# Long convolution by token parity: 256 frequencies for both halves of the spectrum, and two input-projection blocks behind the forward transforms

## Chip, cores and metric

The kernel runs on one NeuronCore of a Trainium2 chip. The metric is the device time of one execution, in microseconds.

## What is computed

A two-layer hybrid trunk runs over 128 context and 512 latent tokens (640 columns). Each layer has one input projection whose columns go to four branches: latent attention (A), a bidirectional gated delta rule (B), a long convolution (C) and differential attention (D). A gated merge and an MLP follow. The change lies in branch C:

```python
def _hyena_branch(u, conv_w, conv_b, filt, d_bias):
    uc = _dwconv_centred(u, conv_w) + conv_b
    x0, x1, v = jnp.split(uc.astype(f32), 3, axis=-1)
    v = v * x1
    h_fwd, h_bwd = filt[:, :HY_W], filt[:, HY_W:]
    h_circ = jnp.concatenate([h_fwd, jnp.zeros((1, HY_W), f32), jnp.flip(h_bwd[1:], axis=0)], axis=0)
    n_fft = 2 * seq
    y = jnp.fft.irfft(jnp.fft.rfft(v, n=n_fft, axis=1) * jnp.fft.rfft(h_circ, n=n_fft, axis=0), n=n_fft, axis=1)[:, :seq]
    return ((y + v * d_bias.astype(f32)) * x0).astype(u.dtype)
```

There are 256 channels. Latents (512 tokens) and context (128) are separate sequences.

## The kernel before, in words

Each engine has its own program, written by hand; semaphores (`signal(...)`, waited on with `.nth(l, n)`) join them, and the order of the code is the order of the work. Both layers run in one loop of depth 2.

The input projection is cut into 24 blocks of 128 output columns. `win_block(l, n)` waits for the block's weights in a ring of four slots (SyncE loads them), then makes 8 x 2 matmuls over all tokens into bank pair `psD[:, n % 2]` of PSUM. Blocks 0 to 5 are the convolution's x0, x1 and v; blocks 6 to 11 are the delta rule's q, k and v. ScalarE copies a block to one of two stages (`evac_conv`), and VectorE makes the short convolution from it (`conv`).

`hyena(l)` of TensorE is the stage in question. Between the first blocks it makes the filter network (L786, L791) and the filter's five token tiles (`windowed`, L776), which VectorE multiplies by a decay window (L1919) and turns into a sum and a difference of the two directions. After block 5 come:

- `gate_input_rows` (L756), small matmuls for the delta rule's gates
- the filter's transform (L811, context L814): for each of five tiles of frequencies and for cosine and sine, matmuls over the token tiles; ScalarE scales each result (L1541, L1542)
- `gate_inputs` (L764), the turning of the values, tokens to partitions (L823), which ScalarE copies out (L1544), and the sums with alternating signs, that is the one frequency at the middle of the circle (L832), whose product VectorE makes (L1944)
- the values' transform (L843, L846); for each tile VectorE makes the complex product with the filter's spectrum (L1951 to L1954)
- the inverse (L854 to L859) into `psD`, with the middle frequency as a term of one row (L856, L859)
- VectorE adds `v * d` and multiplies by x0 (L1960, L1963) and signals `hyena_done`, for which TensorE waits ahead of block 6, since the delta rule's buffers lie over the convolution's in the arena.

Then `gdn(l)` takes blocks 6 to 10 and goes on with the delta rule. GpSimd has nothing to do in the stage. It sends the tables (`dft`) to the arena at the layer's start.

Of the kernel before, what the change touches and what calls it, by code (L numbers as in the profile page):

```python
# [101 lines left out]
DFT, DFT_W = layout([("cs", 4 * 2 * LAT), ("csp", 2 * CTX), ("win", NT * 512), ("z", T)])  # L102
# [5 lines left out]
DVE_LINKS = 225  # L108
# [26 lines left out]
def trunk(nc, ins, outs, links):  # L135
    ctx = ExitStack()
    with ctx:
# [70 lines left out]

        cv = Carve()
# [4 lines left out]
        hspec = cv(NT, 3, 256)  # L214
        yspec = filt
        hprod = cv(2, 512)
        hnyq = cv(2, 256)
        hmul = cv(512)

        sarg, sn, ssin = (hspec.rearrange("p a b c -> p (a b c)")[:, i * T:(i + 1) * T] for i in range(3))  # L220
        dcs = dft[:, 0:4096].rearrange("p (k c f) -> p k c f", k=4, c=2)
        dcsp = dft[:, 4096:4352].rearrange("p (c f) -> p c f", c=2)
        win = dft[:, 4352:4352 + 2560].rearrange("p (t c) -> p t c", t=NT)
        zf = dft[0:33, 4352 + 2560:4352 + 2560 + T]
# [11 lines left out]
        def flat_bout(n):  # L236
            return bout[:, n].rearrange("p c t -> p (c t)")

# [78 lines left out]
        hspec_ps = signal("hspec_ps", NT)  # L317
        hspec_ready = signal("hspec_ready", NT)
        vspec_ps = signal("vspec_ps", NT)
        yspec_ready = signal("yspec_ready", NT)  # L320
        nyq_ps = signal("nyq_ps", 1)
        nyq_ready = signal("nyq_ready", 1)
# [116 lines left out]
        pool_chain = signal("pool_chain", 0)  # L439

        def halves(ap):

            return ap.rearrange("p (s n) -> p s n", s=2)

# [88 lines left out]
        def _(pool):  # L533
# [6 lines left out]
            with pool.Fori(0, DEPTH) as l:  # L540
# [5 lines left out]
                pool.dma_start(x_kept, x[:]).then_inc(x_out.sem, 16)  # L546

# [139 lines left out]
        def _(pe):  # L687
# [64 lines left out]
            def gate_input_rows(l):  # L752

                for k in range(KC):
                    for a, b in SEGS:
                        last = mm(psD[32 * (k % 4):32 * (k % 4) + 32, 0, a:b], p_("wab")[:, k * 32:(k + 1) * 32],  # L756
                                  h[:, k, a:b], start=k < 4, stop=k >= 4)
                last.then_inc(ab_rows_ps.sem, 1)

            def gate_inputs(l):  # L760

                pe.wait_ge(*ab_rows_in.nth(l, 1))
                for t in range(NT):
                    last = mm(psD[:, 0, 768 + t * 16:768 + (t + 1) * 16], ab_rows[:, t * P:(t + 1) * P], c_("pick"),  # L764
                              start=True, stop=True)
                last.then_inc(ab_ps.sem, 1)

            def hyena(l):
# [3 lines left out]
                def windowed(tiles):  # L772
                    for t in tiles:
                        if t >= 2:
                            pe.wait_ge(*filt_out.nth(l, t - 1))
                        mm(psA[:, t % 2, :], ssin[0:64, t * P:(t + 1) * P], p_("w3", slice(0, 64)), start=True,  # L776
# [20 lines left out]
                windowed((2, 3))  # L797
                win_block(l, 5)
                windowed((4,))
                pe.wait_ge(*dense_out.nth(l, 5))  # L800
                gate_input_rows(l)

                pe.wait_ge(*filt_out.nth(l, NT))
                for f in range(NT):
                    if f >= 2:
                        pe.wait_ge(*hspec_ready.nth(l, f - 1))
                    for c in range(2):
                        out = psA[:, f % 2, c * 256:(c + 1) * 256]
                        if f < 4:
                            for k in range(4):  # L810
                                last = mm(out, dcs[:, k, c, f * P:(f + 1) * P], filt[:, k, c, :],  # L811
                                          start=k == 0, stop=k == 3)
                        else:
                            last = mm(out, dcsp[:, c, :], filt[:, 4, c, :], start=True, stop=True)  # L814
                    last.then_inc(hspec_ps.sem, 1)

                gate_inputs(l)
                pe.wait_ge(*hv_ready.nth(l, 1))
                pe.wait_ge(*hspec_ready.nth(l, NT))
                for t in range(NT):  # L820
                    for c in range(2):
                        c0 = tok_cols(t)
                        last = nc.tensor.transpose(psA[:, t // 2, (t % 2) * 256 + c * P:(t % 2) * 256 + (c + 1) * P],  # L823
                                                   hv[:, c, c0:c0 + P], c_("ident"))
                last.then_inc(hvt_ps.sem, 1)
                pe.wait_ge(*hvt_ready.nth(l, 1))

                for s, tiles in enumerate((range(4), (4,))):
                    for i, src in enumerate((filt, hvt)):
                        for n, t in enumerate(tiles):  # L830
                            r = src[:, t, 0, :] if i == 0 else src[:, t, :]
                            last = mm(psA[0:1, 2 + s, i * 256:(i + 1) * 256], c_("alt"), r,  # L832
                                      start=n == 0, stop=n == len(tiles) - 1)
                last.then_inc(nyq_ps.sem, 1)
                pe.wait_ge(*nyq_ready.nth(l, 1))
                for f in range(NT):
                    if f >= 2:
                        pe.wait_ge(*yspec_ready.nth(l, f - 1))
                    for c in range(2):
                        out = psA[:, f % 2, c * 256:(c + 1) * 256]  # L840
                        if f < 4:
                            for k in range(4):
                                last = mm(out, dcs[:, k, c, f * P:(f + 1) * P], hvt[:, k, :],  # L843
# [1837 lines left out]
```

## Time and profile before

| | |
|---|---|
| median of 3 runs | 3245.61 us (3245.35 to 3248.56) |
| profiled execution | 3252.41 us, span 3250.8 us |
| TensorE busy | 3008.2 us, 93% |
| VectorE, ScalarE, GpSimd busy | 31%, 25%, 20% |
| granted TensorE clock, mean | 0.968 |
| chain that ended last | TensorE 87%, VectorE 5%, issue 4%, ScalarE 3% |

The span runs from the first to the last instruction of the profiled execution. In rows of the timeline a bracket tells how long the engine was idle ahead of the instruction and what ended it. A float32 matmul of the program is two records of the trace. All buffers of the arena carry the name `arena`. PE is TensorE, DVE VectorE, ACT ScalarE, POOL GpSimd.

### The profile page before, as it was taken

Reading aid. Unit: us, or ns where it says so; the run is one execution under the profiler, and the core shown is the slowest. Engines: PE = TensorE matmul, PEld = TensorE weight load, DVE = VectorE, ACT = ScalarE, POOL = GpSimd, SP = SyncE. Lnnn points to the kernel's source line nnn. Section 1 sums busy time; section 2 is a strip of 40 time slices with the busy share of each in tenths; the row PEclk is TensorE's granted clock in tenths of the full one; section 3 lists DMA queues with packets and bytes.
Section 4 is the critical chain, followed back from the end, with each engine's and each line's share of the span. In section 5 each row is a group of like instructions: output and inputs, shape, how many; then the busy total and the mean of one; then the engine's idle time right before and its main releaser. Section 6 shows DMA issues by size and latency. Waiting matters only on the chain.

```text
span 3250.8 us, 56532 instructions
## 1 busy us (share of the span) xinstructions
PE 3008.2 (93%) x23424; PEld 2491.9 (77%) x23424; DVE 1013.8 (31%) x1982; ACT 811.7 (25%) x1220; POOL 640.3 (20%) x412
## 2 busy tenths in 40 slices
PE   6998989999999989999998898999998898999997
PEld 3656965777777889999955488557777788999996
DVE  1434722224542121111142365132344322111111
ACT  2113113222232141222230310232222214221222
POOL 0001100311112223333300021021112122333331
PEclk8998999999999999999999999999999999999998
DMA  7110001122123322222330100112211242222221
GB/s 292 33 33 21 4 22 45 67 74 74 60 72 124 105 67 91 92 87 91 94 121 7 52 3 3 50 40 73 85 62 64 73 134 74 91 92 92 85 92 72
DMA packets 56671, 236.60 MB, mean 73 GB/s; under 512 B 6624, under 2 KB 6784, under 8 KB 55136
## 3 DMA queue, kind: packets, MB, share of 16 engines
q1 hardware_dynamic: 53568, 206.67, 19.2%
q0 software_dynamic: 2848, 26.18, 2.2%
q8 instruction: 204, 3.34, 0.4%
q14 instruction: 51, 0.42, 0.0%
HBM read 224.00 MB, written 8.81 MB: 72 GB/s over the span
## 4 chain that ended last, share of the span: by engine, by line
PE 87%; DVE 5%; issue 4%; ACT 3%; DMA 1%; POOL 0%; SPq 0%; DVEq 0%; POOLq 0%; ACTq 0%
PE ps_dense L702 45%; PE ps_dense L695 13%; PE ps_aux L1245 3%; PE ps_dense L1194 2%; PE ps_dense L1266 2%; PE ps_aux L991 2%; PE ps_aux L983 2%; PE ps_aux L971 2%; PE ps_dense L737 1%; PE ps_aux L1194 1%; PE ps_aux L724 1%; PE ps_dense L854 1%; DMA w_ring<-in_w_early 1%; PE ps_dense L1257 1%; PE ps_aux L843 1%
## 5 line engine op out<-in xcount | busy, mean ns | idle before, releaser
L623 POOL TENSOR_TENSOR w_low<-w_ring,w_high 128x1024 fp32r<-128x1024 f32 x208 | 512.9, 2467 | 1102.0 <-ACT w_high L1499 1100.5
L702 PE MATMUL ps_dense<-h_high,w_high 128*128 128x320 f32 x2048 | 496.6, 324 | 64.2 <-DVE rs L2291 22.0
L702 PE MATMUL ps_dense<-h_low,w_high 128*128 128x320 f32 x2048 | 472.9, 313 | 0.0
L702 PE MATMUL ps_dense<-h_high,w_low 128*128 128x320 f32 x2048 | 472.8, 313 | 0.0
L695 PE MATMUL ps_dense<-h_norm,w_ring 128*128 128x512 f32 (+1 forms) x1536 | 436.4, 446 | 15.4 <-ACT h_norm L1520 7.5
L695 PEld LDWEIGHTS ps_dense<-h_norm,w_ring 128*128 128x128 f32 x1536 | 240.9, 196 | 215.3 <-issue 202.8
L702 PEld LDWEIGHTS ps_dense<-h_high,w_high 128*128 128x128 f32 x2048 | 338.7, 191 | 87.4 <-issue 63.9
L1499 ACT ACTIVATE w_high<-w_ring 128x1024 fp32r<-128x1024 f32 x208 | 218.7, 1052 | 540.3 <-PE ps_dense L702 442.8
L702 PEld LDWEIGHTS ps_dense<-h_low,w_high 128*128 128x128 f32 x2048 | 347.9, 191 | 0.0
L702 PEld LDWEIGHTS ps_dense<-h_high,w_low 128*128 128x128 f32 x2048 | 347.7, 191 | 0.0
L702 PE MATMUL ps_dense<-z_high,w_high 128*128 128x320 f32 x1280 | 297.1, 314 | 13.5 <-POOL w_low L623 13.5
L702 PE MATMUL ps_dense<-z_low,w_high 128*128 128x320 f32 x1280 | 293.7, 311 | 0.0
L702 PE MATMUL ps_dense<-z_high,w_low 128*128 128x320 f32 x1280 | 293.6, 311 | 0.0
L702 PEld LDWEIGHTS ps_dense<-z_high,w_high 128*128 128x128 f32 x1280 | 214.5, 189 | 16.9 <-issue 16.9
L702 PEld LDWEIGHTS ps_dense<-z_high,w_low 128*128 128x128 f32 x1280 | 215.5, 189 | 0.0
L702 PEld LDWEIGHTS ps_dense<-z_low,w_high 128*128 128x128 f32 x1280 | 215.4, 189 | 0.0
L2401 DVE SCALAR_TENSOR_TENSOR x_res<-ps_dense,mod,x_res 128x320 f32<-128x320 f32 (+2 forms) x192 | 72.6, 434 | 377.5 <-PE ps_dense L702 377.5
L2456 DVE CAST z_high<-flow 128x640 fp32r<-128x640 f32 x64 | 31.7, 495 | 390.6 <-ACT flow L1818 390.6
L2306 DVE TENSOR_REDUCE att_s<-ps_aux 128x1 f32<-128x640 f32 (+1 forms) x120 | 86.1, 718 | 215.6 <-PE ps_aux L1245 184.1
L1816 ACT ACTIVATE flow<-ps_dense 128x640 f32<-128x640 f32 x64 | 45.1, 705 | 324.7 <-PE ps_dense L702 324.7
L552 POOL TENSOR_TENSOR arena<-arena,con 128x1024 f32<-128x1024 f32 x10 | 23.6, 2359 | 516.8 <-DVE arena L2054 516.8
L1194 PE MATMUL ps_dense<-bout,w_ring 128*128 128x128 f32 (+1 forms) x384 | 115.6, 444 | 0.0
(359 smaller groups left out, 3368.8 us busy)
## 6 DMA issues: line engine op xcount, KB each, us to landing
w_ring<-in_w_mlp SPq DMA_DIRECT2D x128, 512.0 KB, 3.7
w_ring<-in_w_gate SPq DMA_DIRECT2D x64, 640.0 KB, 3.9
w_ring<-in_w_late SPq DMA_DIRECT2D x64, 512.0 KB, 4.6
w_ring<-in_w_early SPq DMA_DIRECT2D x48, 512.0 KB, 3.7
w_ring<-in_w_in SPq DMA_DIRECT2D x48, 512.0 KB, 3.6
w_ring<-in_w_out SPq DMA_DIRECT2D x16, 512.0 KB, 3.6
arena<-in_dft POOLq DMA_DIRECT2D x2, 3776.0 KB, 13.4
par<-in_par POOLq DMA_DIRECT2D x3, 1731.0 KB, 8.3
```

The lines of the kernel that those rows point to most:

```text
L623: g.tensor_tensor(w_low[:, n % 2], ring[:, slot, 0:KC, :], w_high[:, n % 2].bitcast(F32), ALU.subtract).then_inc(w_low_in.sem, 1)
L695: last = mm(out[:, a:b], ring[:, j, k, :], rhs[:, k, a:b], start=k == 0, stop=k == KC - 1)
L702: last = mm(psD[:, b, s * 512:s * 512 + HALF], w_[:, par_, k, :], x_[:, k, s * HALF:(s + 1) * HALF], start=k == 0 and x_ is x_high and w_ ...
L971: last = mm(psA[rows(r), 2 * i, u * 64:(u + 1) * 64], lt[s % 3][rows(r), d, hh, rows(r)], mv, start=True, stop=True)
L983: last = mm(psA[rows(r), 2 * i, u * 64:(u + 1) * 64], xt[i][rows(r), u], wm[i][rows(r), u], start=True, stop=True)
L991: last = mm(psA[rows(r), 2 * i + 1, u * 64:(u + 1) * 64], wm[i][rows(r), u], mv, start=True, stop=True)
L1194: last = mm(out[:, a:c], ring[:, 2 * i % RING, KC + k, :], bout[:, BRANCHES[i // KC], k, a:c], start=k == 0, stop=k == 1)
L1245: last = mm(out[:, a:b], qt, k[:, a:b], start=True, stop=True)
L1266: last = mm(psD[64 * (hh % 2):64 * (hh % 2) + 64, 0, T:T + P], vals[:, k if nk > 1 else 5, hh * 64:(hh + 1) * 64], pt[:, k * P:(k + 1) * P ...
L1499: a(w_high[:, n % 2], ring[:, j, 0:KC, :], ACT.Copy).then_inc(w_high_in.sem, 1)
L2306: link(v.tensor_reduce(small_[:, 2 * m, u:u + 1], src, AX.X, ALU.max, negate=True))
L2401: last = v.scalar_tensor_tensor(out=dst[:, p:q], in0=ps, scalar=gate[:, s:s + 1], in1=dst[:, p:q], op0=ALU.mult, op1=ALU.add)
```

## The change

The 512 latent tokens are split by parity into 256 even and 256 odd ones. Sums over the even tokens (E) and over the odd ones (O) are made at 256 frequencies only. The lower half of the spectrum is E + O; the upper half, at mirrored frequencies, is E - O up to signs. The frequency in the middle is made by alternating sums, one for each parity. The inverse makes even and odd tokens apart, from sums and differences of the two halves of the product.

- The tables become three of 256 x 256 (cosine and sine): `ce`, `co` and `ci`; the filter's rows and windows come in the order even, odd.
- `windowed` takes its last tile ahead of block 5, in a bank of its own; the gate rows go to `psA` instead of `psD`.
- Results of the transform go to `spectrum(0)` (two banks of `psA`) or `spectrum(1)` (`psD[:, 1]`). ScalarE copies the filter's, GpSimd makes sum and difference. Of the values' results ScalarE copies the odd part, VectorE makes sum and difference, the products and their parts, and GpSimd the last sum and difference (`yspec`).
- Blocks 6 and 7 move ahead of the inverse; ScalarE evacuates them there; VectorE's convolutions 6 and 7 stay behind `hyena_done`.
- The inverse goes to `psA`; VectorE writes it by parity.
- The context's transform keeps its form.

Core of the diff:

```diff
+def spectrum(f):
+    return psA[:, 0:2, :] if f == 0 else psD[:, 1].rearrange("p (b n) -> p b n", b=2)
...
 # GpSimd
+for f in range(2):
+    pool.wait_ge(*sums_in.nth(l, f + 1))
+    g.tensor_tensor(hspec[:, f, 0], sums[:, f, :, 0], sums[:, f, :, 1], ALU.add)
+    g.tensor_tensor(hspec[:, f, 1], sums[:, f, :, 0], sums[:, f, :, 1], ALU.subtract).then_inc(hspec_ready.sem, 1)
+for f in range(2):
+    pool.wait_ge(*v_steps.nth(l, 2 * f + 2))
+    g.tensor_tensor(yspec[:, f, 0], parts[:, f, 0], parts[:, f, 1], ALU.add)
+    g.tensor_tensor(yspec[:, f, 1], parts[:, f, 0], parts[:, f, 1], ALU.subtract).then_inc(yspec_ready.sem, 1)
...
 # TensorE
-for f in range(NT):
-    if f >= 2:
-        pe.wait_ge(*hspec_ready.nth(l, f - 1))
-    for c in range(2):
-        out = psA[:, f % 2, c * 256:(c + 1) * 256]
-        if f < 4:
-            for k in range(4):
-                last = mm(out, dcs[:, k, c, f * P:(f + 1) * P], filt[:, k, c, :], start=k == 0, stop=k == 3)
+def transform(f, src):
+    for c in range(2):
+        for e, tab in enumerate((ce, co)):
+            for k in range(2):
+                last = mm(spectrum(f)[:, c, e * 256:(e + 1) * 256], tab[:, k, c, f * P:(f + 1) * P],
+                          src(2 * e + k, c), start=k == 0, stop=k == 1)
+    return last
...
+transform(0, of_filter).then_inc(hspec_ps.sem, 1)
+pe.wait_ge(*dense_out.nth(l, 6))
+transform(1, of_filter).then_inc(hspec_ps.sem, 1)
+pe.wait_ge(*ab_rows_in.nth(l, 1))
+context_transform(of_filter).then_inc(hspec_ps.sem, 1)
+middle(of_filter, 512).then_inc(hspec_ps.sem, 1)
...
+middle(of_values, 768).then_inc(vspec_ps.sem, 1)
+for f in range(2):
+    transform(f, of_values).then_inc(vspec_ps.sem, 1)
+context_transform(of_values).then_inc(vspec_ps.sem, 1)
+pe.wait_ge(*ab_kept.nth(l, 1))
+pe.wait_ge(*v_odd_in.nth(l, 1))
+win_block(l, 6)
+pe.wait_ge(*v_steps.nth(l, 3))
+win_block(l, 7)
...
+        for e, tab in enumerate((ce, ci)):
+            out = psA[:, c, e * 256:(e + 1) * 256]
+            for f in range(2):
+                for r in range(2):
+                    mm(out, yspec[:, f, e, r, cols], tab[:, f, r, :], start=f == 0 and r == 0, stop=False)
+            last = mm(out, ymid[0:1, e, cols], c_("altrow", slice(0, 1))[:, 0:256], start=False, stop=True)
...
 # VectorE
+for f in range(2):
+    dve.wait_ge(*v_odd_in.nth(l, f + 2))
+    v.tensor_tensor(vspec[:, 0], spectrum(f)[:, :, 0:256], v_odd[:, f], ALU.add)
+    last = v.tensor_tensor(vspec[:, 1], spectrum(f)[:, :, 0:256], v_odd[:, f], ALU.subtract)
+    last.then_inc(v_steps.sem, 1)
+    ...
+    v.tensor_tensor(pr, vspec, hspec[:, f], ALU.mult)
+    v.tensor_tensor(pr2[:, :, 0], vspec[:, :, 0], hspec[:, f, :, 1], ALU.mult)
+    link(v.tensor_tensor(pr2[:, :, 1], vspec[:, :, 1], hspec[:, f, :, 0], ALU.mult))
+    v.tensor_tensor(parts[:, f, :, 0], pr[:, :, 0], pr[:, :, 1], ALU.add)
+    v.tensor_tensor(parts[:, f, :, 1], pr2[:, :, 1], pr2[:, :, 0], ALU.subtract).then_inc(v_steps.sem, 1)
```

TensorE's order in the stage before, from the filter's transform on (L811), through the turning (L823) and the middle sums (L832), to the first half of the inverse:

```order
L811 MATMUL ps_aux<-arena 128x256 x32
L814 MATMUL ps_aux<-arena 128x256 x2
L764 MATMUL ps_dense<-con,bout 128x16 x5
L823 MATMUL ps_aux<-con,arena 128x128 x10
L832 MATMUL ps_aux<-arena,con 1x256 x10
L843 MATMUL ps_aux<-arena 128x256 x32
L846 MATMUL ps_aux<-arena 128x256 x2
L854 MATMUL ps_dense<-arena 128x512 x8
L856 MATMUL ps_dense<-con,arena 128x512
L858 MATMUL ps_dense<-arena 128x128 x2
L859 MATMUL ps_dense<-con,arena 128x128
```

The same engine in the changed kernel, from the second group of the filter (L839) to the values' context part (L846); L875 is the turning, L796 the gate inputs, L853 and L854 the middle sums:

```order
L839 MATMUL ps_dense<-arena 128x256 x8
L846 MATMUL ps_aux<-arena 128x256 x2
L853 MATMUL ps_aux<-arena,con 1x256 x4
L854 MATMUL ps_dense<-arena,con 1x256
L870 ISA
L875 MATMUL ps_aux<-con,arena 128x128 x10
L796 MATMUL ps_dense<-con,bout 128x16 x5
L880 REGISTER_ALU
L853 MATMUL ps_aux<-arena,con 1x256 x4
L854 MATMUL ps_dense<-arena,con 1x256
L839 MATMUL ps_aux<-arena 128x256 x8
L839 MATMUL ps_dense<-arena 128x256 x8
```

Each transform has 16 latent matmuls in place of 32, the gate inputs stand behind the turning, and half of the middle sums stand ahead of it. Behind the last matmuls of block 7 (L727), the inverse of the changed kernel reads, context first (L897, L898), then the even and odd tokens (L906, with the one-row term L907):

```order
L727 MATMUL ps_dense<-h_norm,w_ring 128x128
L897 MATMUL ps_aux<-arena 128x128 x2
L898 MATMUL ps_aux<-con,arena 128x128
L897 MATMUL ps_aux<-arena 128x128 x2
L898 MATMUL ps_aux<-con,arena 128x128
L906 MATMUL ps_aux<-arena 128x256 x4
L907 MATMUL ps_aux<-con,arena 128x256
L906 MATMUL ps_aux<-arena 128x256 x4
L907 MATMUL ps_aux<-con,arena 128x256
```

The sixteen 512-column matmuls of the inverse have become sixteen of 256 columns, and they stand behind blocks 6 and 7 instead of ahead of them. VectorE's product of one spectrum tile was (five times a layer):

```order
L1951 TENSOR_TENSOR arena<-ps_aux,arena 128x512 [waits vspec_ps]
L1952 TENSOR_TENSOR arena<-ps_aux,arena 128x512
L132 REGISTER_ALU
L1953 TENSOR_TENSOR arena<-arena 128x256 [waits dve_chain]
L1954 TENSOR_TENSOR arena<-arena 128x256
```

For one of the two groups of latents it is now:

```order
L2008 TENSOR_TENSOR arena<-ps_aux,arena 128x512 [waits middle_and_odd_sums_in]
L2009 TENSOR_TENSOR arena<-ps_aux,arena 128x512
L2011 ISA
L2014 TENSOR_TENSOR arena<-arena 128x1024 [waits hspec_ready,signs_taken_and_parts_ready]
L2015 TENSOR_TENSOR arena<-arena 128x2x256
L2016 TENSOR_TENSOR arena<-arena 128x2x256
L133 REGISTER_ALU
L2017 TENSOR_TENSOR arena<-arena 128x2x256 [waits dve_chain]
L2018 TENSOR_TENSOR arena<-arena 128x2x256
```

More of it reads the arena on both sides, and a wait on GpSimd's `hspec_ready` has come in.

## Rows read from the trace of the kernel before

**Rows 1.** The page, busy time of each engine (share of the span, instructions).
```profile
PE 3008.2 (93%) x23424; PEld 2491.9 (77%) x23424; DVE 1013.8 (31%) x1982; ACT 811.7 (25%) x1220; POOL 640.3 (20%) x412
```

**Rows 2.** Windows, block 5's end to block 8's start: us, PE, PEld, DVE, ACT, POOL, PEclk, DMA.
```profile
122.06:211.70 89.64, 79.12 (x324) 50.30 (x324) 24.25 (x44) 7.98 (x16) 0.00 (x0) 0.96 0.04 12
...
1709.40:1800.65 91.25, 80.73 (x324) 50.94 (x324) 24.25 (x44) 7.97 (x16) 0.00 (x0) 0.94 0.04 12
```

**Rows 3.** Timeline of TensorE, layer 0: start us, us, instruction, count, idle before it.
```profile
123.11 2.40 PE L756 MATMUL ps_dense<-h_norm,par 128*32 128x512 f32 x32
126.95 14.08 PE L811 MATMUL ps_aux<-arena 128*128 128x256 f32 x64 [1.44 <-DVE arena L1922]
140.87 1.03 PE L814 MATMUL ps_aux<-arena 128*128 128x256 f32 x4
141.73 1.18 PE L764 MATMUL ps_dense<-con,bout 128*128 128x16 f32 x10
143.20 1.28 PE L823 MATMUL ps_aux<-con,arena 128*128 128x128 f32 x10 [0.29 <-ACT arena L1542]
145.88 4.48 PE L832 MATMUL ps_aux<-arena,con 128*1 128x256 f32 x20 [1.39 <-ACT arena L1545]
152.08 14.08 PE L843 MATMUL ps_aux<-arena 128*128 128x256 f32 x64 [1.73 <-DVE arena L1945]
...
170.54 8.83 PE L854 MATMUL ps_dense<-arena 128*128 128x512 f32 x16 [3.52 <-DVE arena L1954]
179.30 1.12 PE L856 MATMUL ps_dense<-con,arena 1*128 1x512 f32 x2
180.35 0.71 PE L858 MATMUL ps_dense<-arena 128*128 128x128 f32 x4
181.00 0.48 PE L859 MATMUL ps_dense<-con,arena 1*128 1x128 f32 x2
181.41 7.13 PE L854 MATMUL ps_dense<-arena 128*128 128x512 f32 x16
188.47 1.12 PE L856 MATMUL ps_dense<-con,arena 1*128 1x512 f32 x2
...
192.80 44.92 PE L695 MATMUL ps_dense<-h_norm,w_ring 128*128 128x512 f32 x160 [2.15 <-DVE bout L1963]
```

**Rows 4.** Windows, three of layer 0 and one of layer 1; granted clock third from last.
```profile
141.90:152.10 10.20, 6.79 (x41) 3.61 (x40) 1.81 (x5) 2.46 (x5) 0.00 (x0) 1.00 0.00 0
...
170.50:174.00 3.50, 3.46 (x6) 1.55 (x7) 0.00 (x0) 0.00 (x0) 0.00 (x0) 0.68 0.00 0
...
192.80:196.00 3.20, 3.20 (x6) 1.79 (x7) 0.00 (x0) 0.00 (x0) 0.00 (x0) 0.55 0.00 0
...
1780.00:1784.00 4.00, 3.88 (x6) 1.94 (x7) 0.06 (x1) 0.00 (x0) 0.00 (x0) 0.50 0.00 0
```

**Rows 5.** Timeline of ScalarE, layer 0: evacuations of blocks 6 and 7.
```profile
203.23 0.60 ACT L1490 ACTIVATE stage<-ps_dense 128x512 f32<-128x512 f32 x1 [57.41 <-PE ps_dense L695]
...
211.88 0.60 ACT L1490 ACTIVATE stage<-ps_dense 128x512 f32<-128x512 f32 x1 [7.89 <-PE ps_dense L695]
```

**Rows 6.** Timeline of VectorE, layer 0: gating of the values, product of one spectrum tile.
```profile
127.55 1.49 DVE L1937 TENSOR_TENSOR arena<-arena 128x1284 f32<-128x1284 f32 x1
...
155.84 0.69 DVE L1951 TENSOR_TENSOR arena<-ps_aux,arena 128x512 f32<-128x512 f32 x1 [3.81 <-PE ps_aux L843]
156.45 0.68 DVE L1952 TENSOR_TENSOR arena<-ps_aux,arena 128x512 f32<-128x512 f32 x1
157.16 0.42 DVE L1953 TENSOR_TENSOR arena<-arena 128x256 f32<-128x256 f32 x1
```

**Rows 7.** Timelines of GpSimd and VectorE in the delta rule, layer 0.
```profile
298.09 1.34 POOL L559 TENSOR_TENSOR arena<-arena 128x256 f32<-128x256 f32 x2
...
298.11 1.29 DVE L2081 TENSOR_TENSOR arena<-ps_dense,arena 128x512 f32<-128x512 f32 x2 [0.75 <-ACT arena L1606]
...
306.66 1.28 DVE L2090 TENSOR_TENSOR arena<-ps_dense,arena 128x512 f32<-128x512 f32 x2
```

More of the change, by code:

```diff
@@ L213, in trunk, with table @@
         filt = cv(NT, 2, 256)
[L214 to L224, printed above, removed]
+        at_sums = cv.at
+        sums = cv(2, 2, 2, 256)
+        hspec, hspec_c = cv(2, 2, 2, 256), cv(2, 256)
+        hprod, hprod2 = cv(1024), cv(1024)
+        cv = Carve(at_sums)
+        sarg, sn, ssin = cv(T), cv(T), cv(T)
+        parts = sums
+        flat_filt = filt.rearrange("p t c n -> p (t c n)")
+        yspec = flat_filt[:, 0:2048].rearrange("p (f e r n) -> p f e r n", f=2, e=2, r=2)
+        yspec_c = flat_filt[:, 2048:2560].rearrange("p (r n) -> p r n", r=2)
+        def table(name):
+            a, w = DFT[name]
+            return dft[:, a:a + w]
+        ce, co, ci = (table(n).rearrange("p (k c f) -> p k c f", k=2, c=2) for n in ("ce", "co", "ci"))
+        dcsp = table("csp").rearrange("p (c f) -> p c f", c=2)
+        win = table("win").rearrange("p (t c) -> p t c", t=NT)
+        zf = table("z")[0:33]
+        at_win = DFT["win"][0]
+        v_odd = dft[:, at_win:at_win + 1024].rearrange("p (f c n) -> p f c n", f=2, c=2)
+        vspec = dft[:, at_win + 1024:at_win + 2048].rearrange("p (s c n) -> p s c n", s=2, c=2)
+        ymid = dft[0:1, at_win + 2048:at_win + 2816].rearrange("p (i n) -> p i n", i=3)
         cv = Carve()
@@ new lines, in middle, with of_filter, of_values @@
+                def middle(src, at):
+                    for e in range(2):
+                        for k in range(2):
+                            mm(psA[0:1, 3, e * 256:(e + 1) * 256], c_("alt"), src(2 * e + k, e), start=k == 0, stop=k == 1)
+                    return mm(psD[0:1, 0, at:at + 256], c_("alt"), src(4, 0), start=True, stop=True)
+                def of_filter(t, c):
+                    return filt[:, t, c, :]
+                def of_values(t, c):
+                    return hvt[:, t, :]
@@ L825, in hyena @@
                 last.then_inc(hvt_ps.sem, 1)
+                gate_inputs(l)
                 pe.wait_ge(*hvt_ready.nth(l, 1))
[L828 to L838, printed above, removed]
-                    for c in range(2):
[L840 to L843, printed above, removed]
-                                          start=k == 0, stop=k == 3)
-                        else:
-                            last = mm(out, dcsp[:, c, :], hvt[:, 4, :], start=True, stop=True)
-                    last.then_inc(vspec_ps.sem, 1)
@@ new lines, in hyena @@
+                pe.wait_ge(*yspec_ready.nth(l, 2))
+                for c in range(2):
+                    cols = slice(c * P, (c + 1) * P)
+                    for e, tab in enumerate((ce, ci)):
[4 more added lines that the diff above has]
+                        last = mm(out, ymid[0:1, e, cols], c_("altrow", slice(0, 1))[:, 0:256], start=False, stop=True)
+                    last.then_inc(hy_ps.sem, 1)
@@ L862, in gdn @@
             def gdn(l):
-                for n in range(6, 11):
+                for n in range(8, 11):
                     win_block(l, n)
```

185 lines of the change are left out of this document (108 added, 77 removed).

## Prediction

> **What bounds the kernel now.** I read the page first: TensorE is busy 93% of the span [rows 1], so time is saved where TensorE has less to do or waits less. Next I marked off, in the windows view, the stage that the change touches: from the end of column block 5 to the start of block 8 of the input projection. It takes 89.6 us in layer 0 and 91.3 us in layer 1, with 324 matmul records in both [rows 2]; each matmul of the program is two records. In both layers TensorE is idle for 10.5 us of it.
>
> TensorE's timeline of this stage in layer 0 [rows 3] shows where the 89.6 us go. The small gate rows take 2.4, the filter's transform 14.1, the middle-frequency sums 4.5, the values' transform 14.1, the inverse 20.1 (170.5 to 190.7), and blocks 6 and 7 follow from 192.8. The idle times stand in brackets: 1.44, 0.29, 1.39, 1.73, 3.52 and 2.15 us. The last waits for VectorE to finish the convolution's output; the others wait for evacuations or products between the transforms. Layer 1 has the same six waits. [...]
>
> **The change, part by part, per layer.**
>
> *Forward transforms.* Before, each has 32 matmuls of 256 columns for the 512 latents; now 16 (two groups of frequencies, two kinds, two parities, two tiles). The 64 records take 13.92 us from start to start (126.95 to 140.87), 0.435 us a matmul. Sixteen fewer save 6.96 us; the values' transform has the same form and duration, so it saves 6.96 too. The context's two matmuls stay.
>
> *Inverse.* Before: 20.1 us. Now 16 matmuls of 256 columns in place of 16 of 512. At full clock a 512-column one costs 7.06/8 = 0.88 (181.41 to 188.47), so one of 256 costs 0.44, and 16 cost 7.06. Four middle terms with one row and 256 columns are a form that the trace lacks: the same with 512 columns costs 1.05, with 128 columns 0.41 [rows 3]. I take 0.61, on the line between them, and keep both ends: 2.4 us, from 1.6 to 4.2. The context's part is twice 0.65 + 0.41 = 2.1. Together 11.6, so 8.5 are saved; 1.8 of these come from the slow first half, since no gap stands ahead of the inverse any more.
>
> *Middle sums.* Ten matmuls, 4.48 us, become five behind the filter and five behind the values: nothing. The matmul of window 4 moves ahead of block 5: nothing.
>
> *Waits.* Five idle times sum to 8.4 us. The 1.44 was the filter's last tile, finished by VectorE only after block 5's convolution; it is now finished ahead of block 5. The 0.29 and the 1.73 were behind the filter's scaling and the old middle product. The filter now goes to two banks that are free; the scaling of its context part (0.7 us) lies beside the middle sums (2.2). The 1.39 is ScalarE copying the turned values out of PSUM, from the end of the turns (144.5) to the start of the middle sums (145.88) [rows 3]: the gate inputs (1.18) now run beside it, and 0.3 is left. The 3.52 was VectorE's product for the last frequencies: blocks 6 and 7 now run there. Saved: 8.4 - 0.3 = 8.1. The 2.15 before the next block stays, now ahead of block 8, and I let its slow clock stay too.
>
> *The cover.* Blocks 6 and 7 cost the same wherever they stand (8.65 from one evacuation to the next [rows 5]), 17.3 together, but what they cover must fit. Counting from the end of block 5, TensorE: gate rows to 2.4, filter to 10.2, middle to 12.5, turns to 13.8, gate inputs, values' first group from 17.5 to 21.0, second to 24.4, context 25.3, blocks to 42.6. VectorE starts on the first group at about 22.1, behind a 0.7 us copy by ScalarE. Per group it makes two sums of 512 elements, a product of 1024, and four of 512. From [rows 6]: one of 512 costs 0.61 behind another and 0.69 to its end; 1284 elements cost 1.49, so 1024 cost 1.14 in a row; with the waits between, 5.1 us a group. The context's product is 2.2 (256 elements: 0.42) and the middle product six one-row instructions, 2.5. In all 14.9 us, done at about 37.0. The cover ends at 42.6: 5.6 us to spare. GpSimd's additions of 512 elements cost 1.3 each, as two of 256 do [rows 7], and the last pair ends about 35. On the filter's side they end near 13, long before VectorE asks at 22. So the new work of VectorE, ScalarE and GpSimd costs nothing; without the cover it would cost about 12 us a layer.
>
> *What is late next.* Convolutions 6 and 7 on VectorE wait now for the end of the long convolution and run beside block 8: some 5 us of 8.65. The table's transfer shrinks from 3776 to 3264 KB and was not waited for. The next blocks' weights can come earlier.
>
> *Strides.* Turning every second token and writing every second token cost what their plain forms cost, or at most twice: four 0.69-0.75 us instructions, of which one lies behind the last matmul. That is 0 to 0.8 us a layer; I take 0, since the element counts are the same.
>
> **The sum:** 6.96 + 6.96 + 8.5 + 8.1 = 30.5 us per layer, 61.0 for two. The profiled execution took 3252.4 us (span 3250.8), so it would take 3191.4. The median of the runs is 6.8 lower, 3245.6, so I predict **3184.6 us**.
>
> [...] In [rows 7] VectorE's pair of instructions beside GpSimd's lasts 1.29 us, and the same pair next to none lasts 1.28: no contention, but these read PSUM and SBUF, whereas the new products and sums read two SBUF operands. [...]
>
> **The rivals.**
>
> *The cover is too short.* If products, parts and context sums take longer than 20.5 us instead of 14.9, TensorE waits ahead of the inverse. Against it: every duration has a near row. For it: the two-operand forms beside GpSimd, and long chains with a semaphore between steps. If the chain took twice as long (29.8) it would end at 51.9, and the wait would be 9.3 a layer: 3203. Chance 0.12.
>
> *The clock falls once more per layer.* The stretch of middle sums, turns and gate inputs has matmuls with one output row or 16 columns, and the inverse has more one-row ones. For it: 0.68 in a window after a short idle. Against: 1.00 in the stretch from 141.9 to 152.1, which holds the same work and more idle time [rows 4]. Price: 1.7 us (8.83 against 7.13) to 3.3 a layer, so 3188 to 3191. Chance 0.13.
>
> *The clock does not fall ahead of block 8.* The wait there is 2.1 us, and what precedes it is shorter than before. The five blocks behind it took 44.92 us, 1.7 more than 5 x 8.65; in layer 1 the stage was 1.6 longer still. That gives back about 5.0: 3179.6. Chance 0.11.
>
> *Slower than before.* [...] Chance 0.03.
>
> **How the numbers follow.** The forecast has 0.61. Its own range: one-row matmuls -1.6 to +3.6 for both layers, strides up to 1.6, the wait behind the turned values up to 1.4 more: 3183 to 3191. The range of 8 in 10 adds the case of the clock that stays up and part of the cover's: **3178 to 3200**. A difference of 0.2%, 6.5 us, is about what a measurement of this kernel can tell from none. All cases but the slow one are beyond it: faster 0.96, same 0.01, slower 0.03.
>
> **What would show it.** In the changed profile the stage from the end of block 5 to block 8 should be about 58 us in layer 0 and 60 in layer 1. The 256-column transforms should have 32 records each with means as before; no wait on VectorE or GpSimd ahead of the inverse; one wait near 2.1 us ahead of block 8, with the low clock behind it; 0.3 us ahead of the values' middle sums. A wait ahead of the context's inverse would prove the first rival; a clock under 1 anywhere before block 8 the second. I am wrong if blocks 6 and 7 wait for their bank, or if the transforms' matmuls grow longer than 0.435 us.

## The result and the profile after

| | before | after |
|---|---|---|
| median, four runs each | 3247.09 us (3245.35 to 3250.96) | 3172.53 us (3170.5 to 3175.59) |
| after / before | | 0.977, 95% interval 0.9753 to 0.9787 |
| profiled execution, span | 3250.8 us | 3173.6 us |
| TensorE busy | 3008.2 us | 2953.1 us |

The change saves 74.6 us. The prediction was 3184.6 us with a range of 3178 to 3200: the direction was right, the time is 12.1 us below the prediction and outside its range.

The page of the changed kernel, busy times of the engines and the queue that brings instructions (packets, MB, share):

```profile
PE 2953.1 (93%) x23304; PEld 2462.0 (78%) x23304; DVE 1022.6 (32%) x1984; ACT 812.6 (26%) x1218; POOL 660.2 (21%) x428
q8 instruction: 148, 2.42, 0.3%
```

TensorE has 55.1 us less of work than in [rows 1]. The rest of the 77.2 us of span is idle time. The second row turned out to matter more than any other; in the kernel before it read

```profile
q8 instruction: 204, 3.34, 0.4%
```

TensorE's timeline of the changed stage in layer 0, which answers to [rows 3] (start us, us, instruction, count, idle before it; L788 gate rows, L839 transforms, L853 and L854 middle sums, L875 turning, L796 gate inputs, L727 projection blocks, L897 to L907 inverse):

```profile
124.12 2.40 PE L788 MATMUL ps_aux<-h_norm,par 128*32 128x512 f32 x32
126.45 3.72 PE L839 MATMUL ps_aux<-arena 128*128 128x256 f32 x16
130.01 3.62 PE L839 MATMUL ps_dense<-arena 128*128 128x256 f32 x16
133.46 1.03 PE L846 MATMUL ps_aux<-arena 128*128 128x256 f32 x4
134.42 1.89 PE L853 MATMUL ps_aux<-arena,con 128*1 128x256 f32 x8
...
136.67 1.44 PE L875 MATMUL ps_aux<-con,arena 128*128 128x128 f32 x10
...
139.57 1.89 PE L853 MATMUL ps_aux<-arena,con 128*1 128x256 f32 x8 [0.44 <-ACT arena L1598]
...
141.82 3.72 PE L839 MATMUL ps_aux<-arena 128*128 128x256 f32 x16
...
149.70 17.47 PE L727 MATMUL ps_dense<-h_norm,w_ring 128*128 128x512 f32 x64
167.00 0.61 PE L897 MATMUL ps_aux<-arena 128*128 128x128 f32 x4
...
169.01 1.99 PE L906 MATMUL ps_aux<-arena 128*128 128x256 f32 x8
170.93 0.69 PE L907 MATMUL ps_aux<-con,arena 1*128 1x256 f32 x2
...
181.47 26.22 PE L727 MATMUL ps_dense<-h_norm,w_ring 128*128 128x512 f32 x96 [2.20 <-DVE bout L2049]
```

Two idle times are left where six were: 0.44 us ahead of the values' middle sums and 2.20 us ahead of block 8. Nothing waits ahead of the inverse. The windows from the gate rows to block 8 in both layers, which answer to [rows 2] (us, then busy time of PE, PEld, DVE, ACT, POOL, granted clock, DMA share, GB/s), show full clock:

```profile
124.12:181.47 57.35, 54.71 (x261) 36.74 (x261) 25.18 (x40) 9.43 (x18) 9.98 (x8) 1.00 0.09 28
1673.98:1731.33 57.35, 54.70 (x262) 36.73 (x261) 25.18 (x40) 9.43 (x18) 9.97 (x8) 1.00 0.09 28
```

To find where all of the 77.2 us went, I cut both timelines at instructions that both kernels have: the gate rows, the first matmul of the MLP's loop and the first one behind that loop.

| stretch | before | after | difference |
|---|---|---|---|
| start to layer 0's gate rows | 123.11 | 124.12 | +1.0 |
| gate rows to the MLP loop, layer 0 | 1030.27 | 999.56 | -30.7 |
| the same, layer 1 | 1033.44 | 999.47 | -34.0 |
| MLP loop, layer 0 | 478.39 | 473.63 | -4.8 |
| MLP loop, layer 1 | 478.77 | 473.63 | -5.1 |
| end of loop to layer 1's gate rows | 78.65 | 76.67 | -2.0 |
| end of layer 1's loop to the end | 28.17 | 26.52 | -1.7 |

The changed stage lies in the second and third rows: 64.7 us, where 61.0 were forecast. Of these, 31.1 and 32.7 have been saved by the end of block 10; the remaining 1.0 comes later and is no more than scatter, since layer 1's stretch took 1033.4 us in one profile of the kernel before and 1030.1 in another. The first row is scatter too: the changed kernel's gate rows start at 124.12 us here and at 122.17 and 120.03 in two further profiles. The last four rows, 13.5 us, are in code that the change does not touch. The MLP's loop has four turns. In the kernel before, TensorE is idle at each of the three returns of each loop. Its timeline there:

```profile
1153.38 0.87 PE L702 MATMUL ps_dense<-h_high,w_high 128*128 128x320 f32 x2 [7.69 <-DVE h_low L1879]
...
1276.35 0.53 PE L702 MATMUL ps_dense<-h_high,w_high 128*128 128x320 f32 x2 [1.18 <-issue]
...
1394.85 0.53 PE L702 MATMUL ps_dense<-h_high,w_high 128*128 128x320 f32 x2 [1.69 <-DVE x_res L2401]
...
1512.87 0.54 PE L702 MATMUL ps_dense<-h_high,w_high 128*128 128x320 f32 x2 [1.19 <-issue]
...
1631.77 3.57 PE L737 MATMUL ps_dense<-h_norm,con 128*128 128x512 f32 x7 [2.08 <-ACT h_norm L1506]
```

In the changed kernel the same loop has no such row; its first and last marks are

```profile
1123.68 0.87 PE L734 MATMUL ps_dense<-h_high,w_high 128*128 128x320 f32 x2 [7.69 <-DVE h_low L1940]
...
1597.31 8.92 PE L769 MATMUL ps_dense<-h_norm,con 128*128 128x512 f32 x32 [2.08 <-ACT h_norm L1554]
```

"issue" means that nothing in the profile held TensorE; the middle row names VectorE, but the same data is no wait in the changed kernel. What did come at these moments were packets on the instruction queue q8. In the kernel before nine start in each turn from the second on, 27 in three turns (1271.8 to 1627.0 us), four of them close together around the return: at 1266.6, 1273.5, 1278.1 and 1282.4 us, where the loop returns at 1276.35. In the changed kernel none starts between 1228.7 and 1605.2 us, nor between 2778.5 us and the end of the span. Six turns of nine packets are 54 of the 56 by which q8 fell. The change takes 30 matmuls out of TensorE's program ahead of this loop; each is two records of a matmul and two of a weight load. The trace has 17494 TensorE records ahead of the first loop before and 17374 after: 120 instructions fewer. That gave the theory for the runs below: **where the loop's code stands in TensorE's program decides whether that code is fetched anew in each turn.**

Most of the 3.6 us of the table's last two rows follow right behind the loops. Windows behind the loop of layer 0 and of layer 1, before:

```profile
1631.80:1636.00 4.20, 4.20 (x9) 2.32 (x10) 0.46 (x4) 4.20 (x7) 0.53 (x1) 0.60 0.91 323
3222.70:3226.00 3.30, 3.30 (x6) 1.54 (x7) 0.00 (x0) 3.30 (x6) 0.00 (x0) 0.59 0.00 0
```

and after:

```profile
1597.30:1601.50 4.20, 4.19 (x14) 2.30 (x15) 0.46 (x4) 4.20 (x7) 0.56 (x1) 1.00 0.92 328
3147.10:3150.40 3.30, 3.30 (x12) 1.87 (x13) 0.00 (x0) 3.30 (x6) 0.00 (x0) 1.00 0.00 0
```

A wait of 2.08 us stands ahead of both. Behind it the clock was 0.60 and 0.59 before (in part 0.50, from 1634 to 1636 and from 3224 to 3226 us) and 1.00 after.

### The profile page after: what moved, and what is told of

It reads as the page before. It is cut to its first block, busy times and chain, and to the rows that moved or that the text cites. A ratio compares the mean times of both kernels' runs of the same rounds, so it can differ in the third digit from the quotient of the medians.

```text
span 3173.6 us, 56302 instructions
## 1 busy us (share of the span) xinstructions
PE 2953.1 (93%) x23304; PEld 2462.0 (78%) x23304; DVE 1022.6 (32%) x1984; ACT 812.6 (26%) x1218; POOL 660.2 (21%) x428
## 3 DMA queue, kind: packets, MB, share of 16 engines
q8 instruction: 148, 2.42, 0.3%
## 4 chain that ended last, share of the span: by engine, by line
PE 87%; DVE 5%; issue 4%; ACT 3%; DMA 1%; POOL 0%; SPq 0%; DVEq 0%; POOLq 0%; ACTq 0%
PE ps_dense L734 46%; PE ps_dense L727 14%; PE ps_aux L1293 3%; PE ps_dense L1242 2%; PE ps_dense L1314 2%; PE ps_aux L1039 2%; PE ps_aux L1031 2%; PE ps_aux L1019 2%; PE ps_dense L769 1%; PE ps_aux L1242 1%; PE ps_aux L756 1%; DMA w_ring<-in_w_early 1%; PE ps_dense L1305 1%; DVE att_s L2392 1%; PE ps_dense L1088 1%
## 5 line engine op out<-in xcount | busy, mean ns | idle before, releaser
L727 PE MATMUL ps_dense<-h_norm,w_ring 128*128 128x512 f32 (+1 forms) x1536 | 432.8, 443 | 15.5 <-ACT h_norm L1568 7.5
L727 PEld LDWEIGHTS ps_dense<-h_norm,w_ring 128*128 128x128 f32 x1536 | 239.1, 195 | 213.7 <-issue 205.8
L734 PE MATMUL ps_dense<-z_high,w_high 128*128 128x320 f32 x1280 | 296.8, 313 | 13.5 <-POOL w_low L655 13.5
L734 PEld LDWEIGHTS ps_dense<-z_high,w_high 128*128 128x128 f32 x1280 | 214.5, 189 | 16.9 <-issue 16.9
L1242 PEld LDWEIGHTS ps_dense<-bout,w_ring 128*128 128x128 f32 x384 | 61.8, 191 | 45.9 <-issue 45.9
```

Source lines behind the costliest of these rows:

```text
L727: last = mm(out[:, a:b], ring[:, j, k, :], rhs[:, k, a:b], start=k == 0, stop=k == KC - 1)
L734: last = mm(psD[:, b, s * 512:s * 512 + HALF], w_[:, par_, k, :], x_[:, k, s * HALF:(s + 1) * HALF], start=k == 0 and x_ is x_high and w_ ...
L1242: last = mm(out[:, a:c], ring[:, 2 * i % RING, KC + k, :], bout[:, BRANCHES[i // KC], k, a:c], start=k == 0, stop=k == 1)
```

## The experiments

Most runs concern the place of the loop's code. The last two concern the cover, that is blocks 6 and 7 running while VectorE works, and GpSimd's part in it.

**Three repeats.** Empty TensorE instructions were to shift the program, 136 in the kernel before, 120 and 256 in the changed one. In the expectations "placement" is the theory above, by which the loop's code stays with TensorE (it "fits") or is fetched anew, and its rival is the clock. By placement I expected the kernel before with 136 to be 10 to 13 us faster, 3235, and the changed one with 256 to stay at 3172 to 3174. That supposes that 136 more act like 120 fewer, and 256 more like none, which no trace had shown by then.

```diff
+            for _ in range(136):
+                pe.nop()
             for _ in range(RING):
                 pe.nop().then_inc(block_done.sem, 1)
```

> The kernel before with 136 empty instructions at the start of TensorE's program, where it waits for the first weights: nothing is computed otherwise. [...] Rival, the clock (the shorter stage shifts the phase of the clock's falls): no change, 3247, fetches and idle times as before.

> The changed kernel with 120 empty instructions at the start of TensorE's program, so that the MLP loop stands exactly where it stood before. Placement: 10 to 13 us slower than the changed kernel, 3184, with idle times of 1 to 2 us at the six returns of the loop. Clock: no change, 3172.

> [...] If any added instruction costs time, whatever its place: 1 to 10 us slower.

Measured: 3248.61 us (ratio to before 1.0001, 0.9992 to 1.001), 3174.93 (0.9772, 0.9759 to 0.9785) and 3170.74 (0.9769, 0.9754 to 0.9784). The bare instructions are dropped when the program is built (the trace of the first has 56532 instructions, as before), so these were the two kernels again, and the expectations were not put to the test. As repeats they are worth something: the loop of layer 0 took 478.46 us in the kernel before and 473.63 in the changed one with 256, as in the first profiles, so this difference belongs to the program and not to the execution.

**The code of the kernel before, shifted.** The added instructions now increment a semaphore that nobody waits on at those values, so they stay: the trace has 136 instructions more.

```diff
+            for _ in range(136):
+                pe.nop().then_inc(held_waits.sem, 1)
             for _ in range(RING):
                 pe.nop().then_inc(block_done.sem, 1)
```

> The kernel before with 136 semaphore increments at the start of TensorE's program, where it waits for the first weights; the bare empty instructions of the earlier attempt were dropped when the program was built, so that it was the kernel before once more. [...] Rival, the clock's phase: 3247, fetches and idle times as before.

Measured: 3245.07 us, ratio 0.999 (0.9981 to 0.9999), where by placement I had again expected 10 to 13 us less, 3235. The loops take 473.62 us, the rows at their returns are gone, q8 has 149 packets and none that starts in turns 2 to 4 of layer 0's loop (1282.7 to 1637.9 us). But the whole is hardly faster, since the gate rows start at 131.56 us instead of 123.11: the increments stand ahead of those that release the weights' ring. The loops speak for the theory; the total needs the run further down.

**The changed kernel, shifted back,** by 120 (where the kernel before has its loop) and by 60:

> The changed kernel with 120 such increments, so that the MLP loop stands exactly where it stood before. Placement: 10 to 13 us slower than the changed kernel, 3184, fetches in every iteration and idle times of 1 to 2 us at the six returns. Clock: no change, 3172.

> The changed kernel with 60 increments, the MLP loop halfway between its two places. Placement: either 3172 or 3184, and nothing between, since the loop fits or does not; which of the two is not foretold. Clock: 3172.

Measured: 3192.33 us (0.9827, 0.9814 to 0.984) and 3194.0 us (0.9835, 0.982 to 0.985), both some 20 us slower than the changed kernel. The loops' idle rows are back in both, with 203 packets, 27 of them in turns 2 to 4 of each loop. With 120, TensorE waits at the loops' six returns for 8.3 us: 4.8 us in three waits put down to `x_res` and 3.5 us in three by issue. In the profiled executions the gate rows start 4.8 and 3.3 us later than in the changed kernel; the loops take 9.7 and 9.5 us more, and the stretches behind them 3.6 and 3.4 us more. The run with 60 says that half of the shift is enough.

**The same shifts, hidden.** Here the increments stand behind the instructions that open the ring, so that they run while TensorE waits for its first weights: 136 in the kernel before, 120 in the changed one.

```diff
             for _ in range(RING):
                 pe.nop().then_inc(block_done.sem, 1)
+            for _ in range(136):
+                pe.nop().then_inc(held_waits.sem, 1)
```

> The kernel before with the same 136 empty semaphore increments on TensorE, now behind the four that open the ring, so that they run inside the wait for the first weights and nothing is held up. Place of the code: the MLP loop stands 136 instructions later in TensorE's program; the idle time of 1.2 to 1.7 us at each return of the loop goes, the instruction queue shows about 150 packets instead of 204, block 0 starts at 60 us as in the kernel before, and the time falls by 10 to 15 us, to 3232 to 3237. Rival, that the gain of the earlier padding came from the later start (transfers that fell elsewhere): with the start back at 60 us the time is the kernel before's within 3 us.

> The changed kernel with 120 such increments at the same hidden place, which puts its MLP loop back to where the kernel before has it in TensorE's program. Place of the code: about 203 packets on the instruction queue, the idle time at the loop's returns is back, block 0 starts at 61 to 62 us, and the time rises by 9 to 13 us, to 3181 to 3186, which is the time that the prediction's sum gave. Rival, that the time is lost by the later start alone: 3173 to 3175.

Measured: the kernel before with 136 takes 3239.33 us against 3246.58 for the unchanged one, ratio 0.9973 (0.9962 to 0.9983). The changed kernel with 120 takes 3187.22 us, ratio 0.9814 (0.9801 to 0.9828), against 0.977 without. Adding work that computes nothing makes the one kernel faster by 7.3 us and the other slower by about 14. The profile of the first, beginning and end of layer 0's loop, nothing idle between:

```profile
1156.43 0.87 PE L702 MATMUL ps_dense<-h_high,w_high 128*128 128x320 f32 x2 [7.69 <-DVE h_low L1881]
...
1630.07 5.45 PE L737 MATMUL ps_dense<-h_norm,con 128*128 128x512 f32 x18 [2.08 <-ACT h_norm L1508]
```

and the profile of the second:

```profile
1121.18 0.87 PE L734 MATMUL ps_dense<-h_high,w_high 128*128 128x320 f32 x2 [7.70 <-DVE h_low L1942]
...
1244.12 0.53 PE L734 MATMUL ps_dense<-h_high,w_high 128*128 128x320 f32 x2 [1.16 <-issue]
...
1362.58 0.53 PE L734 MATMUL ps_dense<-h_high,w_high 128*128 128x320 f32 x2 [1.65 <-DVE x_res L2489]
...
1480.60 0.53 PE L734 MATMUL ps_dense<-h_high,w_high 128*128 128x320 f32 x2 [1.20 <-issue]
...
1599.50 10.60 PE L769 MATMUL ps_dense<-h_norm,con 128*128 128x512 f32 x32 [2.08 <-ACT h_norm L1556]
```

Set side by side with the two kernels they are shifts of:

| | loop, layers 0 and 1 | end of loop 0 to the next block 0 | q8 packets |
|---|---|---|---|
| before | 478.39, 478.77 | 15.62 | 204 |
| before, 136 hidden | 473.64, 473.63 | 13.94 | 149 |
| after | 473.63, 473.63 | 13.93 | 148 |
| after, 120 hidden | 478.32, 477.99 | 15.62 | 203 |

The effect is switched on and off by the place of the code alone, in both kernels. The gain in the kernel before is under the forecast 10 to 15 us, because the gate rows still start 3.0 us late (126.08); from there to the end its span is 13.6 us shorter than that of the unchanged kernel. The changed kernel with 120 came out 1 us above the forecast 3181 to 3186. In its profiled execution, the fastest of five (3183.64 us), the loops and the stretch behind the first give 9.0 + 1.7; what makes the other executions up to 5 us slower was not looked for. Neither rival holds: in the kernel before the start came later and the total fell, and in the changed one the start (121.90 us) lies within the 120.03 to 124.12 of its unpadded profiles while the total rose.

**How far from the border, and of what kind it is.** The same hidden edit with 20 and with 256.

> The changed kernel with 20 empty increments. It tells how near the changed kernel stands to the border. If the loop still keeps its code: loops of 473.6 us and about 148 packets, time 3170 to 3176; if 20 instructions are enough to cross the border: loops of 478 us, 203 packets, 3181 to 3188. By the theory of the borders both can be; I hold the first for somewhat likelier, since 20 is a twelfth of the period.

> The changed kernel with 256 empty increments ahead of everything. Theory A, that the place of the MLP loop's code against the borders of the 16 KB packets decides, with a period of some 256 instructions (the changed kernel, and the kernel before with 136 more, which is 256 behind it, keep the loop; 60 and 120 behind it do not): the loops take 473.6 us, no packet is fetched inside them, about 149 packets in all. Theory B, that it is the amount of code ahead of the loop: the loops take 478 us, with 10 packets an iteration, 203 or more in all. The increments may end later than the first weights land, so the start may be later by 10 to 30 us; the loops are read by themselves.

Measured, one execution each: with 20, 3175.77 us; with 256, 3196.8 us, of which 21.2 are a later start (gate rows at 145.29; its first wait, by issue, is 41.2 us long). The loops, which are the point, take 473.63 us in both layers of both. Beginning and end of layer 0's with 256:

```profile
1144.91 0.87 PE L734 MATMUL ps_dense<-h_high,w_high 128*128 128x320 f32 x2 [7.69 <-DVE h_low L1942]
...
1618.54 8.92 PE L769 MATMUL ps_dense<-h_norm,con 128*128 128x512 f32 x32 [2.08 <-ACT h_norm L1556]
```

There are 150 and 149 packets, and in turns 2 to 4 of the loops none starts in either run (1242.8 to 1598.0 and 2792.4 to 3147.6 us with 20, 1263.3 to 1618.5 and 2813.0 to 3168.2 with 256), as with 0; with 60 and 120 it was 27 a loop. Theory B, the amount of code ahead, falls: with 256 instructions more the loop runs without packets again, as it did in the kernel before with 136. There it stands 120 + 136 = 256 instructions behind the place that the changed kernel's has. A packet holds 16 KB (2.42 MB in 148), and a turn that is fetched anew takes nine of them, not the ten of the expectation. Of theory A the runs show that the place decides, at these five shifts, and that 256 more act like none; a period and borders of packets they do not show.

An estimate from the traces' counts: ahead of the loop, some 7310 TensorE records go with 28 packets (577 to 1153 us in the kernel before), about 261 a packet, so that 256 instructions are about one packet. A turn has 840 matmuls, 840 weight loads and 49 other records, 1729 in all, or 6.6 packets of 261. At which places between 20 and 60 and between 120 and 256 the loop changes over, why the place decides, and why nine packets come for a turn of 6.6, was not measured.

**The cover taken away.** Blocks 6 and 7 stand behind the inverse again, and so do ScalarE's evacuations of them; the same work, another order. TensorE's part of the edit:

```diff
 pe.wait_ge(*v_odd_in.nth(l, 1))
-win_block(l, 6)
-pe.wait_ge(*v_steps.nth(l, 3))
-win_block(l, 7)
...
-for n in range(8, 11):
+for n in range(6, 11):
     win_block(l, n)
```

> The changed kernel with blocks 6 and 7 back behind the inverse. My account: TensorE waits for VectorE's and GpSimd's chain ahead of the inverse, from about 25.9 to 39 us behind block 5, 13 us a layer, and the clock falls after it in the inverse, 1.7 us or more: 27 to 32 us slower than the changed kernel, 3200 to 3205. Rival (the chain is short, the move is worth only the old wait of 3.5 us and the clock): 7 to 12 us slower.

Measured: 3213.78 us, ratio 0.9897 (0.9882 to 0.9913), 41 us slower than the changed kernel and slower than the expected 3200 to 3205. Without the order, less than half of the gain of 74.6 us is left. TensorE's timeline in layer 0:

```profile
161.22 1.20 PE L894 MATMUL ps_aux<-arena 128*128 128x128 f32 x4 [13.32 <-DVE arena L2030]
...
164.95 3.78 PE L903 MATMUL ps_aux<-arena 128*128 128x256 f32 x8
168.66 1.22 PE L904 MATMUL ps_aux<-con,arena 1*128 1x256 f32 x2
169.81 3.59 PE L903 MATMUL ps_aux<-arena 128*128 128x256 f32 x8
...
173.95 1.99 PE L903 MATMUL ps_aux<-arena 128*128 128x256 f32 x8
```

The wait for VectorE is 13.3 us. Then the inverse's first half runs at half the clock (granted 0.50 from 164 to 172 us; 3.78 us for what takes 1.99), so that the inverse takes 17.8 us instead of 12.3. The wait and 5.5 us of clock make 19 us in this layer, up to the end of block 10. The expectation had 13 for the wait and only 1.7 "or more" for the clock. Up to the MLP loop the two layers are 15.9 and 20.4 us longer than in the changed kernel, in an execution of 3209.66 us, the fastest of the four; where the rest of the 41 us lies was not located.

**GpSimd out of VectorE's way.** Its last two pairs of additions wait for the end of VectorE's chain.

```diff
 for f in range(2):
-    pool.wait_ge(*v_steps.nth(l, 2 * f + 2))
+    pool.wait_ge(*v_steps.nth(l, 5))
```

> The changed kernel with GpSimd's last two pairs of additions behind all of VectorE's products. If the two engines lock each other out, VectorE's 1024-element product of the second group takes 1.23 us instead of 2.34, its first context sum 0.42 instead of 1.44, and its chain ends 2.1 us earlier; the whole time does not change (3172), since blocks 6 and 7 cover both. If they do not, both stay as long as they are.

Measured: 3174.9 us in its one execution, the changed kernel's time. VectorE's timeline of the changed kernel, the product of 1024 elements for the first and the second group and the context's of 256:

```profile
146.21 0.69 DVE L2008 TENSOR_TENSOR arena<-ps_aux,arena 128x512 f32<-128x512 f32 x1 [6.80 <-ACT arena L1604]
...
147.53 1.23 DVE L2014 TENSOR_TENSOR arena<-arena 128x1024 f32<-128x1024 f32 x1
...
151.21 0.68 DVE L2008 TENSOR_TENSOR arena<-ps_dense,arena 128x512 f32<-128x512 f32 x1
...
152.61 2.34 DVE L2014 TENSOR_TENSOR arena<-arena 128x1024 f32<-128x1024 f32 x1
...
158.90 1.44 DVE L2027 TENSOR_TENSOR arena<-arena 128x256 f32<-128x256 f32 x1
```

GpSimd's timeline beside it:

```profile
151.37 1.28 POOL L576 TENSOR_TENSOR arena<-arena 128x512 f32<-128x512 f32 x1 [14.02 <-DVE arena L2018]
152.60 1.27 POOL L577 TENSOR_TENSOR arena<-arena 128x512 f32<-128x512 f32 x1
...
158.79 1.26 POOL L577 TENSOR_TENSOR arena<-arena 128x512 f32<-128x512 f32 x1
```

And VectorE's in this run, the same instructions without GpSimd beside them:

```profile
149.22 1.23 DVE L2014 TENSOR_TENSOR arena<-arena 128x1024 f32<-128x1024 f32 x1
...
154.40 0.43 DVE L2027 TENSOR_TENSOR arena<-arena 128x256 f32<-128x256 f32 x1
```

Two instructions that start up to 0.11 us behind a GpSimd addition last about as long as both together: 2.34 us, where 1.27 and 1.23 make 2.5, and 1.44, where 1.26 and 0.43 make 1.7. Apart they take 1.23 and 0.43. That the two shut each other out costs VectorE's chain 2.1 us a layer (1.11 + 1.01), all under the cover. The expectation's durations are met: 1.23, 0.43 and an unchanged total.

## Why the prediction was wrong, and where it was right

**The step that failed** is the first: "Next I marked off, in the windows view, the stage that the change touches", and with it a sum that has no term outside that stage. It treated 30 matmuls fewer as time only. They are code as well, and by their number the MLP's loop, 900 us further on, came to stand where it is not fetched anew. That is worth 13.5 us: 9.9 in the loops, shown by the shifts in both directions, and 3.6 at their ends, where the clock no longer falls; this followed the shifts at every loop's end but one. With the shift undone (120 hidden) the changed kernel takes 3187.22 us, 2.6 above the predicted 3184.6 and inside the range. That it comes so near is in part luck: the inverse takes 0.7 us a layer more than forecast, and in one layer of this run the 1.7 us that the forecast has for the clock behind the wait is missing. The signs stood in the profile of before and were not read: q8's 204 packets, and the waits "by issue" at the returns of a loop.

The range failed with it: it was made from the unknown costs of the stage alone.

**The stage, term by term,** counted in layer 0 from the start of the gate rows (124.12):

| ends of | forecast | measured |
|---|---|---|
| the filter's transforms | 10.2 | 10.3 |
| turning | 13.8 | 13.8 |
| the values' first group | 21.0 | 21.3 |
| blocks 6 and 7 | 42.6 | 42.9 |
| inverse, its length | 11.6 | 12.3 |
| wait ahead of block 8 | 2.15 | 2.20 |
| start of block 8 | 56.3 | 57.35 |

- *Forward transforms:* two of 3.6 to 3.7 us for 8 matmuls each, as forecast; nothing longer than 0.45 us a matmul.
- *Inverse:* 0.7 longer. A group of four 256-column matmuls took 1.92 from start to start, 0.48 each; I had halved the 0.88 of the 512-column ones. The one-row matmul cost 0.63 (170.93 to 171.56) where 0.61 was taken between bounds of 0.41 and 1.05 (the straight line between them gives 0.62).
- *Strides:* next to nothing, where 0 was taken. VectorE's instruction that writes every second token takes 0.75 us (at 174.21), as its plain form did (at 181.59 before), and the ten turning matmuls take 1.17 us from the first start to the last instead of 1.01.
- *Waits:* 0.44 instead of 0.3 ahead of the values' middle sums; the other four are gone.
- *Cover:* VectorE began at 22.1, as forecast. Its chain is 16.9 us long (146.21 to 163.1) instead of 14.9; the lock is 2.1 of that, and without it the chain took 14.7 (gpsimd_late). The spare time was 3.9 us of the forecast 5.6. The prediction's sum had no term for the lock, since [rows 7] had no pair with two SBUF operands on both engines; of GpSimd's four additions two were in the way, at 2.34 against 1.23 us and 1.44 against 0.43. What the cover is worth was put too low: "about 12 us a layer" is 19 in layer 0, of which 5.5 are the clock.
- *Clock behind the 2.2 us wait:* "I let its slow clock stay" did not hold in the profiled execution, where three blocks took 26.22 us at full clock (granted 1.00); this rival had 0.11. But in seven of the eight other profiles that have blocks 6 and 7 ahead of the inverse, these three blocks took 27.9 us in one layer or both. The two repeats of the changed kernel are among them, with 27.9 in both layers. So the same program has both, the term is 1.7 us where it comes, and it came in 11 of the 18 layers of the nine profiles. This is the row of the repeat with 120 bare instructions:

```profile
179.51 27.90 PE L727 MATMUL ps_dense<-h_norm,w_ring 128*128 128x512 f32 x96 [2.20 <-DVE bout L2051]
```

- *Layer 1:* 34.0 saved where 30.5 were forecast. The forecast read layer 0 for both, though [rows 2] had layer 1's stage 1.6 longer, and its five blocks behind the wait took 46.55 against 44.92. Some of the 34.0 is scatter behind the stage: up to the end of block 10 layer 1 saves 32.7, and in the repeat of the kernel before its stretch to the MLP loop is 3.3 shorter.
- *A slip of its own:* "about 58 us in layer 0 and 60 in layer 1" does not come from the sum, which gives the same length in both, 56.3 to block 8's start from the gate rows. Measured were 57.35 in both.

Of the 16.2 us by which the span lies under the forecast 3189.8, the loops and their ends are 13.5, the two stretches from the gate rows to the MLP loop 3.7, and a start 1.0 later goes the other way; the last two are about the size of the scatter between executions of one program. The rival of the short cover and the second fall of the clock did not come, nor a time slower than before.

## What to carry over

In a kernel whose busiest engine runs loops of long bodies (here 1729 instructions a turn), an edit also moves all code behind it, and that can cost or save time beside its own terms (here 13.5 of 77.2 us): look at the instruction queue's packet count and for idle time at loop returns in both profiles, and before crediting a surprise to the edit, shift the code by some instructions that compute nothing. Put the wide, independent matmuls where the long dependent chain of another engine runs: here taking that order away cost 41 of the 75 us, over a quarter of it by the clock (5.5 and 6.1 us in the two inverses). Read every layer's own rows when a sum is doubled.

## What the runs showed of the hardware

- Whether the loop's body is fetched anew, by nine 16 KB packets a turn, went by its place in the program: with 0, 20 and 256 instructions added ahead of the changed kernel's no packet starts in turns 2 to 4 of either loop, with 60 and 120 it is 27 a loop. In the kernel before it is 27 with 0 and none with 136. Fetched anew, each return costs 1.1 to 1.7 us of idle time, 4.4 to 5.1 us a loop of four turns.
- After the same 2.08 us wait at the loop's end, TensorE's clock was granted at 0.60 and 0.59 in the two layers of the kernel before and at 1.00 in the changed one. Wherever a profile shows the stretch behind a loop, it is 1.7 us longer behind loops with such returns (15.62 against 13.94 us, or 10.60 against 8.92) but for one, layer 1 of the changed kernel with 120 hidden, and never behind the others. Whether the short idle times of the turns do it, or only make it likelier, stays open; it was not tried apart.
- VectorE's instructions with two SBUF operands, begun up to 0.11 us behind a GpSimd addition with two, lasted about as long as both in turn: 2.34 us where 1.27 and 1.23 make 2.5, and 1.44 where 1.26 and 0.43 make 1.7; apart they took 1.23 and 0.43. VectorE's sums with one operand in PSUM were not held up: the one that starts at 151.21 us takes 0.68 beside GpSimd's addition that starts at 151.37, and one of the same form that starts at 157.51 takes 0.69 beside the addition at 157.56.
